# Summing squares on VectorE before one ones-matmul, in the query norms of a two-block transformer kernel

## What is computed

```
def rms_norm(x, gain):                       # first block
    return x * lax.rsqrt(jnp.mean(x * x, axis=-1, keepdims=True) + EPS) * gain

q = (h @ xq[l]).reshape(B, S, 4, 256)        # cross attention, 4 heads of 256
q = rms_norm(q, xq_gain[l])                  # a mean over 256 channels, per head

qa, ka, va, cq, ckv, kr, gates = jnp.split(h @ w_in, IN_SPLITS, axis=-1)
q = heads(_rmsnorm(cq, g_q) @ w_uq, 8)       # latent queries: a mean over 768 channels
kv = heads(_rmsnorm(ckv, g_kv) @ w_ukv, 8)   # latent keys and values: over 256
```

## Time and profile before

| | |
|---|---|
| time, median of 3 runs | 2401.75 us |
| the runs | 2397.44, 2401.75, 2402.91 us |
| the profiled execution | 2397.45 us, its span 2395.5 us |
| mean granted TensorE clock | 0.995 |
| busy: TensorE matmul | 2325.3 us, 97% of the span |
| busy: VectorE, ScalarE, GpSimd | 912.2, 874.8, 1102.9 us |

### The profile page before, as it was taken

How to read it: one execution, slowest core, us unless ns; L and a number is a source line. 1 busy time by engine, 2 the same in 40 slices (tenths; PEclk the granted TensorE clock), 3 DMA queues, 4 the chain that set the end, 5 groups by cost and what they waited for, 6 DMA issues and landing times.

```text
span 2395.5 us, 33550 instructions
## 1 busy us (share of the span) xinstructions
PE 2325.3 (97%) x12124; PEld 1891.2 (79%) x12124; DVE 912.2 (38%) x1561; ACT 874.8 (37%) x1240; POOL 1102.9 (46%) x1356
## 2 busy tenths in 40 slices
PE   7999999899999999999999999999999999999997
PEld 6778687588888888888888888877766787888886
DVE  3324532498877771110111045234126554111113
ACT  3354543444233453212211234255434534422222
POOL 3333455099877764333333334333332054555544
PEclk9999999999999999999999999999999999999999
DMA  4222132256555531111211122222221022222222
GB/s 155 92 76 85 53 123 81 95 181 200 189 193 186 193 124 62 62 62 62 70 62 62 62 80 69 71 93 69 79 81 48 1 97 67 98 91 97 97 97 97
DMA packets 66604, 231.37 MB, mean 97 GB/s; under 512 B 7216, under 2 KB 9520, under 8 KB 66352
## 3 DMA queue, kind: packets, MB, share of 16 engines
q1 hardware_dynamic: 50656, 180.02, 21.9%
q10 hardware_dynamic: 15824, 49.55, 6.1%
HBM read 226.66 MB, written 2.10 MB: 95 GB/s over the span
## 4 chain that ended last, share of the span: by engine, by line
PE 60%; POOL 20%; issue 17%; DVE 2%; ACT 0%; POOLq 0%; DVEq 0%; ACTq 0%
PE ps L1783 46%; POOL WLO L343 20%; PE ps L2317 4%; PE ps L1818 1%; PE ps L2431 1%; PE ps L2444 1%; PE ps L2259 1%; PE ps L2288 1%; PE ps L2302 1%; PE ps L2432 1%; PE ps L2274 0%; PE ps L1804 0%; PE ps L1800 0%; PE ps L1799 0%; PE ps L2403 0%
## 5 line engine op out<-in xcount | busy, mean ns | idle before, releaser
L343 POOL TENSOR_TENSOR WLO<-RAW,WHI 128x256 fp32r<-128x256 f32 x1340 | 1087.5, 844 | 1248.7 <-ACT WHI L378 1248.0
L1783 PE MATMUL ps<-HLO,WHI 128*128 128x512 f32 (+2 forms) x1840 | 612.6, 367 | 5.7 <-DVE Y L1519 2.1
L1783 PE MATMUL ps<-HHI,WLO 128*128 128x512 f32 (+2 forms) x1840 | 605.3, 363 | 0.0
L1783 PE MATMUL ps<-HHI,WHI 128*128 128x512 f32 (+2 forms) x1840 | 604.2, 362 | 0.0
L378 ACT ACTIVATE WHI<-RAW 128x1024 fp32r<-128x1024 f32 x335 | 354.4, 1059 | 663.0 <-DMA RAW<-in_stream_dram 655.3
L1783 PEld LDWEIGHTS ps<-HLO,WHI 128*128 128x128 f32 (+1 forms) x1840 | 318.7, 188 | 69.0 <-issue 4.6
L1783 PEld LDWEIGHTS ps<-HHI,WHI 128*128 128x128 f32 (+1 forms) x1840 | 317.8, 188 | 58.9 <-issue 3.6
L1783 PEld LDWEIGHTS ps<-HHI,WLO 128*128 128x128 f32 (+1 forms) x1840 | 318.3, 188 | 55.8
L1378 DVE TENSOR_TENSOR SF<-SF,ps 128x512 f32<-128x512 f32 (+1 forms) x66 | 51.2, 777 | 495.5 <-PE ps L1783 486.3
L1783 PE MATMUL ps<-GLO,WHI 128*128 128x512 f32 (+1 forms) x704 | 231.6, 364 | 1.9 <-POOL WLO L343 1.9
L1783 PE MATMUL ps<-GHI,WLO 128*128 128x512 f32 (+1 forms) x704 | 231.5, 364 | 0.0
(11 more groups left out here) (373 smaller groups left out, 2887.9 us busy)
## 6 DMA issues: line engine op xcount, KB each, us to landing
RAW<-in_stream_dram SPq DMA_DIRECT2D x335, 512.0 KB, 3.2
ADA<-in_ada_dram ACTq DMA_DIRECT2D x72, 512.0 KB, 4.3
BM<-in_bias_dram ACTq DMA_DIRECT2D x8, 448.0 KB, 3.6
DECAY<-in_decay_dram ACTq DMA_DIRECT2D x4, 512.0 KB, 4.4
out_dram<-X SPq DMA_DIRECT2D x8, 256.0 KB, 2.2
X<-in_x_dram SPq DMA_DIRECT2D x2, 512.0 KB, 5.6
X<-in_x_dram ACTq DMA_DIRECT2D x2, 512.0 KB, 6.6
C<-in_mem_dram ACTq DMA_DIRECT2D x1, 1024.0 KB, 5.6
```

The lines of the kernel that those rows point to most:

```text
L343: op = nc.gpsimd.tensor_tensor(WLO[:, slot(u), k:k + 2], RAW[:, slot(u), k:k + 2], WHI[:, slot(u), k:k + 2].bitcast(F32), ALU.subtract)
L1783: mm = nc.tensor.matmul(out, w, x[:, k, tok], start=(k == 0 and n == 0), stop=(k == kt - 1 and n == 2))
```

## The change

VectorE adds squares elementwise, and TensorE then needs one ones-matmul for the sum. In the cross attention, `query_add` adds the two tiles of squares of a head in place in SQ[:, 0]; the sum of the second head of a turn is issued one unit (a pair, in the second turn of "xq") later, and that of the last head after the first score matmuls. As `normed` is shared, the last sum of the first turn of "dq" moves a unit later as well. In the latent queries a cleared accumulator ACCQ takes the six squares one after another, and one matmul sums it.

```
-         ("a1", KD, _to_h), ("ckv", 2, _to_h), ("cq", 6, _to_h), ("p3", KD, _to_x + ("px",)), ("a4", KD, _to_h), ("p5", KD, _to_x + ("px",))]
+         ("a1", KD, _to_h), ("ckv", 2, _to_h), ("cq", 6, _acc), ("p3", KD, _to_x + ("px",)), ("a4", KD, _to_h), ("p5", KD, _to_x + ("px",))]
...
                     def root(j):
                         g, lane = (4 // per) * i, j // per
-                        act.wait_ge(s(tag + "_ms"), 4 * i + (j + 3))
+                        act.wait_ge(s(tag + "_ms"), g + (lane + 3))
...
-                        act.wait_ge(s(tag + "_ms"), 4 * i + (j + 1))
+                        act.wait_ge(s(tag + "_ms"), 4 * i + (j + 1) if per == 1 else 2 * i + (j // 2 + 2))
...
-            norm2("cq", 6, [(lambda k: ps[:, CQ_BANKS[k]], 0, S)], S, 768, SQQ, RSQ, TNQ, lambda k: wait_unit(UNIT["cq"] + k), CQHI)
+            for k in range(6):
+                wait_unit(UNIT["cq"] + k)
+                square("cq", SQQ, k, k, [(ps[:, CQ_BANKS[k]], 0, S)])
+            norm2("cq", 6, [(None, 0, S)], S, 768, SQQ, RSQ, TNQ, None, CQHI)
...
+            def query_add(h):
+                dve.wait_ge(s("xq_sq"), 2 * h + 2)
+                V.tensor_tensor(SQ[:, 0], SQ[:, 0], SQ[:, 1], ALU.add).then_inc(s("xq_add"), 1)
...
+            query_add(0)
             for h in range(3):
                 query_scale(h)
+                query_add(h + 1)
...
+            clear(ACCQ[:])
+            for k in range(6):
+                add_square("cq", ACCQ[:], SQQ, k, k)
...
-                def turn(i):
+                def turn(i, carried=None):
                     def total_of(j):
-                        pe.wait_ge(s(tag + "_sq"), 4 * i + (j + 1))
-                        nc.tensor.matmul(ps[:, 4 + (j // per) % 2, 0:n], ones, sq[:, j % 2, 0:n], start=(j % per == 0),
-                                         stop=(j % per == per - 1)).then_inc(s(tag + "_ms"), 1)
+                        if j % per < per - 1:
+                            return
+                        pe.wait_ge(*(s(tag + "_sq"), 4 * i + (j + 1)) if per == 1 else (s(tag + "_add"), 2 * i + j // 2 + 1))
+                        nc.tensor.matmul(ps[:, 4 + (j // per) % 2, 0:n], ones, sq[:, j % 2 if per == 1 else 0, 0:n], start=True,
+                                         stop=True).then_inc(s(tag + "_ms"), 1)
...
                         if j:
                             total_of(j - 1)
+                        elif carried:
+                            carried()
-                    if i < iters - 1 or not held:
-                        total_of(3)
-                    else:
-                        return lambda: total_of(3)
+                    return lambda: total_of(3)
...
+                if n == 0:
+                    last_query()
...
-            sums2("cq", 6, S, SQQ)
+            pe.wait_ge(*norm_at("ckv", "ln", 1))
+            sum_of("cq", ACCQ[:], 6, tiles=6)
```

More of the change, by code:

```diff
@@ L208, in build @@
         (SQQ,), _ = region(q_at + 4 * S * 10, ("SQQ", [P, 2, S], F32))
+        (ACCQ,), _ = region(q_at + 4 * S * 14, ("ACCQ", [P, S], F32))
         (MK, MV, COSQ, SINQ, MQA), _ = region(h_at, ("MK", [P, 8, N2], F32), ("MV", [P, 6, S], F32), ("COSQ", [P, S], F32),
@@ L1843, in spin, with sum_of @@
                     nc.tensor.matmul(ps[:, bank, 0:P], const[:, ONES], const[:, IDENT], start=True, stop=True)
-            def sum_of(tag, acc, bank=7, wait=0, idle=0):
+            def sum_of(tag, acc, bank=7, wait=0, idle=0, tiles=KD):
                 spin(idle, wait)
-                pe.wait_ge(*norm_at(tag, "acc", KD + 1))
+                pe.wait_ge(*norm_at(tag, "acc", tiles + 1))
                 width = acc.shape[-1]
@@ L1939, in turn @@
                             total_of(j - 1)
-                    if i < iters - 1 or not held:
-                        total_of(3)
-                    else:
-                        return lambda: total_of(3)
+                        elif carried:
+                            carried()
+                    return lambda: total_of(3)
+                rest = None
                 for i in range(iters):
-                    rest = turn(i)
-                return rest
+                    rest = turn(i, rest)
+                if held:
+                    return rest
+                rest()
             def project(tag, u0, x, first):
@@ L2099, in _ @@
             pe.wait_ge(s("w_out_x"), KD + 4)
-            normed("xq", UNIT["xq"], 2, 2, S, const[:, ONES], SQ, (HHI, HLO), x_tok, ready=lambda k: (norm_at("n2", "hi", k + 1), norm_at("n2", "lo", k + 1)),
-                   after=lambda j: (key_total(3), pe.wait_ge(s("xk_q"), 3)) if j == 0 else pe.wait_ge(s("xk_q"), 4) if j == 2 else None)
+            last_query = normed("xq", UNIT["xq"], 2, 2, S, const[:, ONES], SQ, (HHI, HLO), x_tok, ready=lambda k: (norm_at("n2", "hi", k + 1), norm_at("n2", "lo", k + 1)),
+                   after=lambda j: (key_total(3), pe.wait_ge(s("xk_q"), 3)) if j == 0 else pe.wait_ge(s("xk_q"), 4) if j == 2 else None, held=True)
             pe.wait_ge(s("xq_q"), 7)
```

## The result

| | before | changed |
|---|---|---|
| median of 17 runs each | 2397.44 us | 2403.14 us |
| the runs | 2394.63 to 2402.91 | 2400.22 to 2409.64 |
| the profiled execution, its span | 2397.45, 2395.5 | 2400.22, 2398.4 |
| mean granted TensorE clock | 0.995 | 0.993 |

The ratio is 1.0026, with a 95% interval of 1.0018 to 1.0034: **slower by 0.26%**, some 6 us. The time lies in the predicted range (2400.5 to 2410.5). It is a loss just beyond 0.2%, where the forecast had put the likeliest case just inside. The page's head and its chain answer to the earlier trace rows.

A forecast was written before the change was run, and what follows sets the result against it. TensorE carries 60% of the chain, so a dropped matmul pays only where TensorE goes on at once. 1.95 - 0.1 + 1.2 + 1.15 = +4.2 on 2401.75 gives 2406 us (small loss, 0.44), range 2400.5 to 2410.5.

The forecast's parts named there:

- Ahead of unit 2: Cross attention: the sum of tile 0 goes, -0.87 us.
- Unit 2 to unit 3: Head 0's one sum waits for VectorE's add, queued behind the last keys; TensorE idles 1.46 us, net +0.6.
- Unit 3 to the pair: Cross attention: both sums leave, -1.83 us; head 0's root and scaling are covered by unit 3.
- The pair to unit 6: Head 1's sum now stands directly ahead of unit 6, which waits for its root and scaling: 3.93 for 1.65, +2.28 us.
- Unit 6 to unit 7: Cross attention: one sum before and after, its add already done, 0 us.
- The end: After unit 7, head 3 is scaled later, at U + 6.0 and not U + 5.04: +0.9 us.
- dq: Turn's end in dq: one of two sums leaves (0.96 back) and stands 0.87 later, -0.1 us.
- The low clock at unit 6: The 3.1 us wait ahead of unit 6 brings one low clock spell: +1.2 us (0 to 3.0).
- the low clock lasts: Rival: a second low spell follows, unit 6 pays 3.0 and ukv's first step 0.4 more: +6.4, 2408 us; chance 0.40.
- The latent queries: Latent stage: adds +0.25, sum at low clock +0.6, ukv's first step +0.3; together +1.15 us (-0.4 to +2.8).
- The add chain: Latent stage: six adds, 3 x 1.0 beside GpSimd and 3 x 0.78, end at 1747.35: +0.25 us (-0.4 to +1.3).
- The sum at low clock: Latent stage: after TensorE's idle from 1742.8 to 1747.4 the one sum runs at low clock, +0.6 us.

The follow-up runs named there:

- kernel 2: The changed kernel with the latent queries as before, so the query edit alone: 2404.13 us, ratio to before 1.0033.
- kernel 3: The changed kernel with 24 unread ones-matmuls ahead of the wait for ACCQ, to hold the clock: 2404.69 us, ratio to before 1.0035.
- Kernel 4: The changed kernel with head 1's sum behind the first of the pair's eight tiles, not behind the pair: 2401.22 us, ratio to before 1.0017.
- 5: The changed kernel with 12 unread ones-matmuls between head 1's sum and unit 6: 2403.42 us, ratio to before 1.0020.
- kernel 9: kernel 3 with ScalarE squaring the first tile straight into ACCQ, so five adds and not six: 2403.48 us, ratio to before 1.0027.
- Kernel 6: The changed kernel with VectorE's add of head 0 ahead of the last keys: 2404.01 us, ratio to before 1.0024.
- 7: The changed kernel with latent queries as before, head 0's add first, head 1's sum in the pair, last head by two sums: 2397.04 us, ratio to before 0.9998.
- 8: 7 with the wait for the last keys moved ahead of unit 3 and the last head's second sum ahead of the first score: 2394.97 us, ratio 0.9995.
- kernel 1: The kernel before with the edit of the latent queries alone (adds into ACCQ, one sum): 2398.79 us, ratio to before 1.0003.

## Why the prediction was right, point by point

**Ahead of unit 2** (-0.87): held; in the changed kernel no sum stands there.

**Unit 2 to unit 3** (net +0.6): 2.52 - 0.87 - 0.87 = +0.78. The idle time was put at 1.46, counted from the start of unit 2's last matmul plus 0.23; counted so it is 382.42 - 380.84 = 1.58 (the row's 1.43 leaves out the end of that matmul). It came so near by two misses that cancel, which is luck: the add took 0.68 and not 1.0, but the last keys ended 0.5 later against TensorE's unit 2 than taken. In the other kernels with this code (2, 3, 4, 5, 9) the row's idle time is 1.51, 1.34, 1.42, 1.29 and 0.98. Kernel 6 adds what the step left out: the add was one hold, TensorE's own wait for the keys, ahead of the same sum, the next.

**Unit 3 to the pair** (-1.83): exact, with head 0's root and scaling hidden by unit 3.

**The pair to unit 6** (+2.28): 4.03 - 1.65 = +2.38. Kernel 4 shows the cause: the same sum some 9 us earlier in the pair, and the step is 0.

**Unit 6 to unit 7** (0): 0.88 and 0.87. Only in kernels 4, 7 and 8, where unit 6 no longer waits, is the add of head 2 late (0.43, 0.59 and 0.27).

**The end** (+0.9): +1.0. **dq** (-0.1): the total of its last tile comes at 182.83 against 182.91, -0.1.

These add up to -0.87 + 1.65 - 1.83 + 2.38 + 1.0 - 0.1 = +2.2, where the steps as forecast gave 1.95 - 0.1.

**The low clock at unit 6** (+1.2): it comes, but not always. The changed kernel, 3, 6 and 9 have a low spell in unit 6 and a second one in the first scores, kernel 2 with the same wait has neither. In windows of 2 us the granted clock of the four goes down to 0.50 to 0.56 in unit 6 and to 0.50 to 0.52 in the first scores; that of kernel 2 is 1.00 in each from 404 to 436. Over the five executions with this wait and no filler at it (changed, 2, 3, 6, 9) the stage has 17 low spells, 3.4 each; over the two with the code of before 5, that is 2.5. One more spell, some 1.4 us, is close to the 1.2 taken. The rival "the low clock lasts" was right in that two spells follow the wait, and wrong that unit 6 pays for both: the second falls into the scores.

**The latent queries** (+1.15, from -0.4 to +2.8): the term that was mis-sized. The root is 2.07 late. The add chain was put at +0.25 and measured +1.07 (kernel 3). Its working was "3 x 1.0 + 3 x 0.78", the first three adds beside GpSimd. The first row below has the adds from 1746.6 on, with the fourth, which began at 1746.09; the second has GpSimd's four instructions (shortest, median and longest in ns):

```profile
L1077 DVE TENSOR_TENSOR ACCQ<-ACCQ,SQQ x3: 692/693/1025, 1746.1 to 1748.4; 128x512 f32<-128x512 f32 x3
L344 POOL TENSOR_TENSOR WLO<-RAW,WHI x4: 735/1168/1172, 1742.4 to 1745.4; 128x256 fp32r<-128x256 f32 x4
```

The working took GpSimd's time from the kernel before, 2.79. Beside the adds it took 4.13, to 1746.57, so four adds and not three ran beside it. From start to start, the first four took 0.95, 1.13, 1.13 and 1.13, together 4.34 where 3.78 was taken, and the last two 1.84 where 1.56 was taken. Behind GpSimd an add took 0.69. Ahead of the last add stand 0.46 of idle and not 0.10, although its square had ended by 1747.81; what held it is open. ScalarE waits for the add that frees a buffer (it idles 0.25 to 0.82 ahead of each of the last four squares, ended by ACCQ), but every square from the second on had ended 0.26 or more before its own add started, so the adds set the pace and not the squares. The four adds beside GpSimd took 3.92 together, four at 0.69 would take 2.76: by an estimate from these rows the hold-up alone is 1.16, about all that the chain lost. No run here has the adds without GpSimd beside them.

The sum at low clock was put at +0.6 and measured +1.0; two records took 2.04, at 456 two in a dense run of eight took 1.6. In the +1.0 there is also 0.1 more from the last add to the sum. Ukv's first step was put at +0.3 and measured 0.
In the 5.89 us of idle that took the place of the sums the granted clock fell from 1.00 (1743 to 1745) to 0.50 (1746 to 1755, with the whole sum in it); before, with the sums in the wait, it was 1.00 from 1742 to 1754 (1748 to 1750 is in the earlier trace rows).

**The sum.** +2.2 for the queries and dq, +2.1 for the latent stage and about +1.4 for one more low spell make +5.7. The medians differ by 5.7, but that the two agree so well is in part luck: the split between spells and other causes rests on few executions, and by the times alone the query edit costs 0.33% (kernel 2) and the latent edit 0.03%, which is no difference (kernel 1). Nor does the one profiled execution give this balance: its span is 2.9 longer, with +4.7 in the two stages and +1.7 between the 169th and the 201st convert, and 3.5 less in the rest. The forecast's +4.2 was too small by 0.9 in the latent stage, 0.4 in the steps and 0.2 in the clock. The predicted 2406 came out 2.9 above the median because it was put on 2401.75, the median of three runs; over 17 it is 2397.44. A base 4.3 too high and an effect 1.5 too small cancel in part, which is luck. On the right base the range would be 2396.2 to 2406.2, and the median lies in that as well. Two bounds are not quite what their terms give: the forecast's own range ends at 2406.6 (2407 stands there) and the whole range at 2408.15 + 0.45 + 1.65 = 2410.25 (2410.5 stands there). And the loss, forecast just inside 0.2%, fell just outside. Its size is nearer that of the rival with +6.4, its cause is the forecast's.

## What to carry to other kernels

A sum that leaves a busy engine is worth its time only where that engine would go on; where it filled a wait, its removal gains nothing and can cost the clock (here it fell to 0.50 in 5.89 us of idle, and was 1.00 there before). When a short instruction is postponed, ask who reads its result: one ones-matmul of 0.87 us, moved behind the work that hid its root and scaling, cost 2.4 us, and moved into that work nothing beyond its own 0.87 (1.19 in kernel 4). Replacing parallel work (squares and sums on two engines) by a string of in-place adds puts every link on the path. And where the new work runs beside another engine's that it holds up, the time of that other engine is not the old one: here 2.79 became 4.13, and four links in place of three were slow ones (1.03 and not 0.69).

## What was not expected of the hardware

**TensorE's pace at a granted clock of 1.00.** From 1200 to 1250 and from 1300 to 1350 us TensorE is busy without a gap in all kernels, on work that no edit touches. One window of the kernel before, and then the same of kernel 9 (the columns as in the earlier trace rows); it is alike from 1300 to 1350:

```profile
1200.00:1250.00 50.00, 50.00 (x291) 43.72 (x290) 5.73 (x6) 8.02 (x8) 16.99 (x25) 1.00 0.19 64
```

```profile
1200.00:1250.00 50.00, 50.00 (x285) 43.32 (x284) 5.73 (x6) 8.03 (x8) 15.98 (x24) 1.00 0.19 64
```

291 matmuls in 50 us against 285: 2% slower, both at 1.00. Kernel 1 has 284 in the first of these windows and 290 in the second, kernels 7 and 8 have 290 and 285. From the 169th to the 201st convert kernel 9 takes 7.0 us longer than the kernel before, kernel 1 3.6, and all ten take between 1.1 and 7.0 longer. So two profiles can differ by more than the whole effect of this change, in a stage that it doesn't concern. As each kernel was profiled once, it is not shown whether this belongs to an execution or to a kernel; kernels 3 and 9 have the same code there (+1.4 and +7.0), and kernel 8 has +3.6 without being slower than before. Five of the changed kernel's 17 runs lie between 2408.2 and 2409.6, the other twelve between 2400.2 and 2405.8, and the granted clock of the five, 0.991 to 0.992, is nearly that of the twelve, 0.991 to 0.993. Whether this pace is the reason can't be said, as no such run was profiled. What sets the pace is open.

**GpSimd beside VectorE's adds.** The same four instructions took 2.79, 4.13 in the kernel with six adds and 3.69 in that with five. One of them took 0.73 alone and 1.17 beside an add, and an add 1.03 in place of 0.69.
Both grow longer side by side, by 0.3 to 0.4 us per instruction here; what makes them do so is not shown. The rows do not show them taking turns for whole instructions: alone, each starts 0.69 or more behind the one before (an add takes 0.69, and the four subtractions of the earlier trace rows come every 2.79 / 4 = 0.70), which would make 1.38 or more for an add and a subtraction in turn, and side by side they came every 1.13.
